# First block's attention: splits and modulation tiles placed by the unit of attention

## The reference

```python
def hybrid_layer(x, c, w_mod, b_mod, g_pre, w_in, ...):
    mod = jax.nn.silu(c) @ w_mod + b_mod
    shift, scale, gate = jnp.split(mod[:, None, :], 3, axis=-1)
    h = rms_norm(x, g_pre) * (1 + scale) + shift
    proj = h @ w_in
    q, k, v, g_att, u, g_lru, merge = jnp.split(proj, split_at, axis=-1)
    y_a = (dilated_attention(q, k, v) * jax.nn.silu(g_att)) @ w_pa
    ...
# dilated_attention: 3 groups x 4 heads of 128, windows (128, 1), (512, 4), (2048, 16);
# softmax of each group's band, groups mixed by their denominators
# second block, twice: mod_x = silu(c) @ ada_w[l] + ada_b[l], mod_c = silu(c_ctx) @ ada_w[l] + ada_b[l], ...
```

## Time and profile before

| | us |
|---|---|
| median of 3 runs (2217.7 to 2224.73) | 2219.04 |
| profiled execution | 2221.63 |
| its span | 2219.8 |
| TensorE busy with matmuls | 2067.8 (93%) |
| VectorE busy | 1271.8 (57%) |
| ScalarE busy | 797.8 (36%) |
| share of the chain that ended last: TensorE, VectorE, ScalarE, DMA | 74%, 12%, 7%, 2% |

### The profile page before, as it was taken

How to read it: one execution, slowest core, us unless ns; L and a number is a source line. 1 busy time by engine, 2 the same in 40 slices (tenths; PEclk the granted TensorE clock), 3 DMA queues, 4 the chain that set the end, 5 groups by cost and what they waited for, 6 DMA issues and landing times.

```text
span 2219.8 us, 26153 instructions
## 1 busy us (share of the span) xinstructions
PE 2067.8 (93%) x11000; PEld 1756.8 (79%) x11000; DVE 1271.8 (57%) x1674; ACT 797.8 (36%) x1105; POOL 88.4 (4%) x89
## 2 busy tenths in 40 slices
PE   5999999998999898899999999999888889999998
PEld 5978777776777787788888888888777677888886
DVE  7465765756755695736645455464558555343343
ACT  4433334475243255424212121131525533232231
POOL 0000000000050000011000000001200000000001
PEclk9999999999998999999999999999999999999999
DMA  8533523522422531112323332232342212222222
GB/s 296 204 142 114 202 83 116 182 88 97 188 78 94 159 82 61 67 58 95 126 95 114 107 114 102 102 136 86 114 140 77 76 67 76 95 95 95 95 97 75
DMA packets 52821, 249.17 MB, mean 112 GB/s; under 512 B 6016, under 2 KB 10256, under 8 KB 34272
## 3 DMA queue, kind: packets, MB, share of 16 engines
q1 hardware_dynamic: 50816, 242.41, 31.6%
q0 software_dynamic: 592, 2.46, 0.3%
q10 hardware_dynamic: 1296, 2.63, 0.3%
HBM read 235.41 MB, written 12.06 MB: 111 GB/s over the span
## 4 chain that ended last, share of the span: by engine, by line
PE 74%; DVE 12%; ACT 7%; issue 4%; DMA 2%; POOL 0%; SPq 0%; ACTq 0%; DVEq 0%; POOLq 0%
PE banks L1707 62%; ACT whi_f L1829 2%; DVE small L1265 1%; DVE wlo_f L2011 1%; PE banks L607 1%; PE banks L616 1%; PE banks L1730 1%; PE banks L1731 1%; PE banks L1732 1%; PE banks L496 1%; DVE aconv L1177 1%; DVE prob L1285 1%; DMA mvr<-in_mst 1%; DVE mvr L2031 1%; PE banks L487 1%
## 5 line engine op out<-in xcount | busy, mean ns | idle before, releaser
L1707 PE MATMUL banks<-hxh,whi_f 128*128 128x512 f32 x1440 | 587.2, 408 | 47.8 <-DVE hxl L2050 14.9
L1707 PE MATMUL banks<-hxh,wlo_f 128*128 128x512 f32 x1440 | 571.2, 397 | 0.0
L1707 PE MATMUL banks<-hxl,whi_f 128*128 128x512 f32 x1440 | 570.6, 396 | 0.0
L2011 DVE TENSOR_TENSOR wlo_f<-raw_f,whi_f 128x2048 fp32r<-128x2048 f32 x133 | 305.7, 2298 | 215.0 <-ACT whi_f L1829 214.9
L1829 ACT ACTIVATE whi_f<-raw_f 128x2048 fp32r<-128x2048 f32 x133 | 253.8, 1908 | 310.3 <-PE banks L1707 291.7
L1707 PEld LDWEIGHTS banks<-hxh,whi_f 128*128 128x128 f32 x1440 | 275.1, 191 | 112.6 <-issue 42.9
L1707 PEld LDWEIGHTS banks<-hxh,wlo_f 128*128 128x128 f32 x1440 | 274.7, 191 | 60.1
L1707 PEld LDWEIGHTS banks<-hxl,whi_f 128*128 128x128 f32 x1440 | 275.3, 191 | 58.1 <-issue 1.9
L1707 PE MATMUL banks<-fxh,whi_f 128*128 128x512 f32 x512 | 202.5, 396 | 2.2 <-DVE cT L1395 1.1
L1395 DVE SCALAR_TENSOR_TENSOR xT<-banks,small,xT 128x512 f32<-128x512 f32 x80 | 59.5, 750 | 252.4 <-PE banks L1707 252.3
L1707 PE MATMUL banks<-fxh,wlo_f 128*128 128x512 f32 x512 | 201.3, 393 | 0.0
(11 more groups left out here) (316 smaller groups left out, 3170.9 us busy)
## 6 DMA issues: line engine op xcount, KB each, us to landing
raw_f<-in_wst SPq DMA_DIRECT2D x133, 1024.0 KB, 4.9
mvr<-in_mst SPq DMA_DIRECT2D x120, 512.0 KB, 5.8
stack<-qk_parts SPq DMA_DIRECT2D x48, 192.0 KB, 6.9
x_kept<-xT SPq DMA_DIRECT2D x2, 2048.0 KB, 8.6
raw_f<-in_wst SPq DMA_DIRECT2D x8, 384.0 KB, 6.0
xT<-x_kept SPq DMA_DIRECT2D x2, 1536.0 KB, 8.8
qk_parts<-qk_h SPq DMA_DIRECT2D x3, 768.0 KB, 3.4
qk_parts<-qk_l SPq DMA_DIRECT2D x3, 768.0 KB, 4.9
```

The costliest lines, as they stand in the source:

```text
L1707: last = pe.matmul(o, w[:, k, c, :], r[part][:, k, :], start=(k == order[0] and w is wh and part == 0), stop=(k == order[-1] and w is wl))
L2011: dve.tensor_tensor(wlo[r][:], raw[r][:], whi[n % 2 if n > N_FIRST else n][:].bitcast(F32), ALU.subtract).then_inc(w_lo, 1)
```

## The change

`places(n, late)` gives the steps i of chunk n that lie five (late) or two (early) places behind the scores of a unit. From chunk 7 on `split(n + 1)` is done inside chunk n, at its first late place (step 2 where there is none), by ScalarE and VectorE alike; before, that split stood after the steps of chunk n - 1. After chunk 23 both programs do `split(25)`, as before. The tiles of a chunk take its late and early places in rising order (3, 8 and 13 before chunk 7 and where there is no late place). In VectorE's program of a step the order is: attention, tile, split. SyncE's, GpSimd's and TensorE's programs are the same.

```diff
@@ -139,6 +139,27 @@
 
 def unit_values(u):
     return unit_scores(u) + 12
+
+
+def places(n, late):
+
+
+    at = [unit_scores(u) + (5 if late else 2) for u in range(16)]
+    return [g - 16 * (n - FILLED) for g in at if 0 <= g - 16 * (n - FILLED) < 16]
+
+
+def split_place(n):
+
+
+    return (places(n, True) + [2])[0]
+
+
+def tile_places(n):
+
+
+    if n < FILLED or not places(n, True):
+        return 3, 8, 13
+    return sorted(places(n, True) + places(n, False)) + [15]
 
 
 VECS = [("b_mod", 24), ("g_pre", 8), ("conv_w", 32), ("conv_b", 8),
@@ -1916,16 +1937,19 @@
                     act.activation(l_e, l_abs, ACT.Exp, scale=-1.0).then_inc(lru_e, 1)
                 for i in range(16):
                     attend_act(act, 16 * (n - FILLED) + i)
+                    if n >= FILLED and i == split_place(n):
+                        split(n + 1)
                     if i == 8:
                         (u_out if n >= C_U else evict)(n, 0)
                 (u_out if n >= C_U else evict)(n, 1)
                 if n in (0, 2):
                     split(4 + n // 2)
-                if n > 3:
+                if 3 < n < FILLED - 1:
                     split(n + 2)
                 if n == 5:
                     act.wait_ge(ld_c2, 32)
                     act.activation(c2b[:], c2b[:], ACT.Silu).then_inc(silu_c, 1)
+            split(C_GL + 1)
             act.wait_ge(at_out, 16)
             for k in range(4):
                 act.activation(ath[:, k, :], att[:, k, :], ACT.Copy).then_inc(ath_done, 1)
@@ -2153,16 +2177,19 @@
                 for i in range(16):
                     attend_dve(dve, link, 16 * (n - FILLED) + i)
                     for k, t in enumerate(MV_SLOTS.get(n, ())):
-                        if i == 5 * k + 3:
+                        if i == tile_places(n)[k]:
                             modulation((t,), mv_sb[:])
+                    if n >= FILLED and i == split_place(n):
+                        split(n + 1)
                     if n >= C_U and i == 10:
                         convolved(2 * (n - C_U))
                 if n >= C_U:
                     convolved(2 * (n - C_U) + 1)
-                if n > 3:
+                if 3 < n < FILLED - 1:
                     split(n + 2)
                 if n == 15:
                     softplus()
+            split(C_GL + 1)
             for k in range(4):
                 dve.wait_ge(ath_done, k + 1)
                 dve.tensor_tensor(atl[:, k, :], att[:, k, :], ath[:, k, :].bitcast(F32), ALU.subtract
```

## The result

The changed kernel takes 2229.2 us, median of 12 runs (2225.1 to 2237.05), against 2218.83 of the kernel before in the same 12 rounds: 10.4 us slower, ratio 1.0047 with a 95% interval of 1.0033 to 1.0061, which is 7.3 to 13.5 us. The forecast was 13.8 us more, with 2223 to 2240 as the range. The profiled execution took 2230.46 us and has a span of 2228.6 us, 8.8 more than the one before.

A forecast was written before the change was run, and what follows sets the result against it. TensorE sets the time, so only its waits (15.1 us in chunks 7 to 23) or a lowered clock count. Losses of 26.7 less gains of 12.9 give 13.8 us slower: 2219.0 + 13.8 = 2232.9, range 2223 to 2240.

The forecast's parts named there:

- Loss 1: Chunks 8, 13, 18: tile at step 0 holds the scale until its landing; 3 x 3.9 = 11.7 us.
- Loss 2: Halved TensorE clock after the long waits in chunks 8, 13 and 18; 3 x 2.7 = 8.1 us.
- Loss 3: Chunks 9 and 19: split too late for the next chunk; 4.8 us, plus 1.6 of clock.
- Loss 4: Chunk 10: split too late for the first matmul of chunk 11; 0.5 us.
- Gain 1: Chunks 22 and 23: waits behind the splits and the low clock after them go; 3.5 and 3.7 us.
- Gain 2: Two waits for ScalarE's copy behind the split's high half, at 156.05 and in chunk 20, go; 3.6 us.
- Gain 3: Small waits of the transposes in chunks 7, 9, 12, 17 and 19 shrink; together 2.1 us.
- Rival 1: The new waits don't lower the clock: only 4.1 us slower, 2223.1; chance 9%.
- Rival 2: The waits grow on each other: 19.8 us slower, 2238.8, or beyond; chance 5%.
- Rivals 3 and 4: rival 3, and a fourth: no change in effect, since VectorE runs ahead of TensorE anyway, 2219; chance 2%.
- rival 3: Step 0 tiles land in time: 12.9 us faster with splits hidden too, 6.0 without; chance 4%.

The follow-up runs named there:

- the tiles issued earlier: Changed kernel with only SyncE's order edited: tiles of chunk n + 1 issued ahead of the weights of chunk n + 3; 2209.7 us, ratio 0.9949.
- the tiles alone: Kernel before with the tiles at their new places and the splits at the old ones; 2234.27 us, ratio 1.0061.
- the kernel with one tile moved: Kernel before with only the first tile of chunk 8 moved from step 3 to step 0; 2224.68 us, ratio 1.0017.
- the repair: Changed kernel with the split put ahead of the tile at step 11 of chunks 9 and 19; 2227.37 us, ratio 1.0022.
- the tile of step 0 at step 3: Changed kernel with one tile each in chunks 8, 13 and 18 moved from step 0 to step 3; 2210.52 us, ratio 0.9957.
- these two splits alone: Kernel before with only the splits of chunks 23 and 24 moved, to step 5 of chunk 22 and step 3 of chunk 23; 2213.82 us, ratio 0.9956.

## Why the prediction was right, point by point

The size first. From chunk 7 to 23 the profile has 8.4 us more (chunk 7 begins 1.1 us later in the trace after, the work behind chunk 23 is 9.5 us later), forecast were 13.8. By steps:

- **Loss 1, the tile at step 0.** Forecast 3 x 3.9 = 11.7. Waits of 4.39, 4.66 and 4.88 for three of 0.8: 11.6. Right in place, size and cause; the tiles issued earlier show that it is the landing, the tiles alone that it needs nothing of the splits.
- **Loss 2, the clock behind it.** The mechanism was right, the size not: 3 x 2.7 = 8.1 forecast, 2.2 + 2.4 + 1.8 = 6.4 measured. The price is not a fixed one for a length of wait: 4.41 in the kernel with one tile moved cost 1.6 (the clock was at half for 3.4 us, from 0.8 after the wait's end), 4.39 in the changed one 2.2. In the profile of the tiles alone the same three waits cost 1.4, 2.4 and 1.6.
- **Loss 3, the late split.** 2.4 each forecast, 2.34 and 2.35 measured. The order of one tile and the split decides it, as the repair shows. Its clock loss, put in as one of two, came in neither in this profile: 1.6 too much in the sum. It came in one of two with the tile of step 0 at step 3 and in both with the tiles issued earlier, so one of two is what the three profiles give together.
- **Loss 4, chunk 10.** 0.5 forecast, 0.39 measured.
- **Gain 1, chunks 22 and 23.** Waits of 0.3 and none were forecast, 0.28 and none came, with no low clock. The kernel with these two splits alone is faster by more than their 7.2, though its interval reaches down to 6.
- **Gain 2, the copy at the edge.** 3.6, both waits gone.
- **Gain 3, the small ones.** Forecast 2.1, measured 1.8. Chunk 12's wait fell from 1.98 to 1.47, as forecast within 0.1. Chunks 7 and 17 keep 0.57 and 0.73 of their 1.22 and 0.94, where I had left 0.9 in all, and chunk 19's 0.45 is gone; chunk 9, which I had named too, has no wait in the row before. The lowered clock that I had left in place in chunk 12 is gone as well, 1.6 more of gain. That the shorter wait did this is not shown: in two other kernels the full 1.98 is there without a lowered clock (below).

So against this profile the forecast was 4.9 too high by three terms of the clock, 1.7 + 1.6 + 1.6, and 13.8 - 4.9 = 8.9 stands beside the profile's 8.4. Each wait at a place that was worked out came within 0.4 us of what was measured. The waits and their causes were right by the working; what the clock cost behind each was a matter of the single execution, and how near the sum came owes something to luck. Rival 1 (no clock loss) is refuted by the 0.50 behind the long waits, though after 2.34 and 2.35 the clock stayed up in this profile. Rival 2 did not happen: the losses did not grow on each other. Rivals 3 and 4 fell with the three waits in the trace; rival 3's condition, a landing in time, was made by hand in the tiles issued earlier, and gave 11 us less than before where 6.0 stood for it. What it had too low are the waits: 9.7 of the 15.1 us are gone, since with the landings earlier the three waits of 0.8 go too (2.3), and so do all of chunk 12's (1.6 beyond the 0.4) and the rest of the small ones (0.9).

The other kernels' profiles show that a wait near 2 us does not settle the clock by its length or its place. Chunk 12's 1.98 is followed by half the clock in the kernel before (3.3 us from 198.5), and by the full one in the kernel with one tile moved. From these transposes to the values it is 4.4 us before, 2.9 there:

```profile
202.60 1.50 PE L496 MATMUL banks<-pt,vb 128*128 128x128 f32 x12
```

```profile
204.60 0.87 PE L487 MATMUL banks<-consts,s_sb 128*128 128x128 f32 x6 [1.98 <-DVE s_sb L537]
...
207.47 1.50 PE L496 MATMUL banks<-pt,vb 128*128 128x128 f32 x12
```

And chunk 10's 2.34, behind which the clock stayed up in the changed kernel, is followed by half of it with the tiles issued earlier (TensorE's timeline, then the stretch):

```profile
155.75 0.55 PE L1755 MATMUL banks<-whi_f,hxh 128*128 128x256 f32 x1 [2.34 <-issue]
```

```profile
155.60:158.90 3.30, 3.15 (x15) 0.50 0.96 400
```

In chunks 7 to 23 of all twelve profiles there are 19 waits of 1.98 to 2.47 us; behind 12 of them the clock is at half for 3.3 to 3.4 us, behind 7 it is not. What decides between the two, and between 3.4 and 6.8 us behind the long waits, stays open. The 2 us between the timed 10.4 and the profile's 8.4 lie within the interval.

## What to carry to other kernels

Before work is put between two steps of a chain in an engine's queue, look at what it waits for itself: its own 2.3 us fitted into the gap, its transfer's landing 6 us after a chunk's end did not, and three such places turned a gain of 10 us into a loss of 10. Move the transfer's issue together with its use: the tiles' new places alone cost 13 us, their earlier issue alone gave nothing, and in the changed kernel it gave 22. And when a job of the next stage is put off, add up all that stands ahead of it between its place and its due time: here the order of one tile and one split decided over 2.0 us at each of two places (2.34 and 2.35 became 0.33).

## What the runs showed of the hardware

Behind a wait of TensorE in chunks 7 to 23 the granted clock was at half or at full. It was at half behind each of the ten waits of 4.4 to 4.9 us in the profiles of the changed kernel, of the tiles alone, of the one tile and of the split ahead of its neighbour, and never behind one of 1.81 or less. In between its length did not settle which: 1.98, 2.34, 2.35 and 2.47 stand on both sides, sometimes at the same place of two kernels, and one of 2.62 later in the kernel left it at full. A wait near 2 us is therefore worth between nothing and 1.6 us beyond itself, one of 4.4 to 4.9 between 1.4 and 2.4 by the rows from transposes to values. The Trainium skill's page "TensorE: Matmul & The Clock Gate", section "Terms", puts the penalty at half of the throttled time; by it the 4.5 us from 134.5 cost an estimated 2.2, and so it was measured.
